# A two-layer hybrid decoder trunk: small matmuls of layer 1's head pairs regrouped between dense matmuls

## The reference

```python
p = h @ w_in
q = p[..., :768].reshape(B, S, 12, 64)
k = p[..., 768:1536].reshape(B, S, 12, 64)
v = p[..., 1536:2304].reshape(B, S, 6, 128)
q = rope(rmsnorm(q, q_norm), positions)
k = rope(rmsnorm(k, k_norm), positions)
...
# for each block of 128 queries, causal
s = einsum('bhqd,bhkd->bhqk', qblk, kh) * 64 ** -0.5
pr = softmax(s).reshape(B, 6, 2, 128, S)
a = pr[:, :, 0] - lam * pr[:, :, 1]
o = einsum('bhqk,bhke->bhqe', a, vh)
...
o = rmsnorm(o, subln) * (1.0 - lambda_init)
```

## Time and profile before

| what | us |
|---|---|
| median of 3 timed runs | 1314.48 (1314.1 to 1315.12) |
| the profiled execution | 1307.47 |
| its span | 1305.4 |
| TensorE busy | 1260.0, 97% |
| GpSimd busy | 722.3, 55% |
| VectorE busy | 609.6, 47% |
| ScalarE busy | 331.2, 25% |

### The profile page before, as it was taken

The page is one execution under the profiler, slowest core; times in us unless marked ns, Lnnn a source line. Parts: engine busy times, 40 slices in busy tenths (PEclk is TensorE's granted clock), DMA queues, the critical chain, the costliest instruction groups (busy, mean ns, idle before and its releaser), DMA issues.

```text
span 1305.4 us, 15225 instructions
## 1 busy us (share of the span) xinstructions
PE 1260.0 (97%) x5762; PEld 1008.4 (77%) x5762; DVE 609.6 (47%) x792; ACT 331.2 (25%) x659; POOL 722.3 (55%) x428
## 2 busy tenths in 40 slices
PE   8999999989999999999999999988999999999999
PEld 6787676658888888888887677766888888888887
DVE  6952522557434233313376888854743313331331
ACT  6422323462221001100122444455222101100110
POOL 6866522316666666666665434322666666666664
PEclk9999999989999999999999999988999999999999
DMA  6323211012323222322233232210222232233322
GB/s 247 97 97 99 95 33 49 33 33 97 105 96 97 97 96 96 97 97 96 77 102 112 65 98 65 82 33 25 97 88 96 96 97 96 96 96 97 97 76 100
DMA packets 34331, 115.85 MB, mean 89 GB/s; under 512 B 4333, under 2 KB 4846, under 8 KB 34158
## 3 DMA queue, kind: packets, MB, share of 16 engines
q1 hardware_dynamic: 32544, 111.16, 26.1%
q10 hardware_dynamic: 1742, 4.10, 1.1%
HBM read 110.00 MB, written 2.10 MB: 86 GB/s over the span
## 4 chain that ended last, share of the span: by engine, by line
PE 87%; DVE 7%; ACT 4%; issue 1%; POOL 1%; DMA 0%; ACTq 0%; SPq 0%; DVEq 0%; POOLq 0%
PE PS L1348 85%; DVE acc L912 2%; DVE nmB L1282 1%; POOL w_lo L467 1%; DVE nmB L1281 1%; DVE xT L1170 1%; DMA xT<-in_x_t_dram 0%; PE PS L1712 0%; DVE Al L1108 0%; ACT tmp L510 0%; DVE Hl L922 0%; ACTq L765 0%; ACT V L695 0%; DVE PS L1279 0%; POOL w_hi L464 0%
## 5 line engine op out<-in xcount | busy, mean ns | idle before, releaser
L464 POOL TENSOR_SCALAR w_hi<-w_raw 128x1024 fp32r<-128x1024 f32 (+1 forms) x205 | 215.5, 1051 | 551.3 <-PE PS L1348 550.7
L467 POOL TENSOR_TENSOR w_lo<-w_raw,w_hi 128x1024 fp32r<-128x1024 f32 (+1 forms) x205 | 499.1, 2435 | 17.1
L1348 PE MATMUL PS<-Hh,w_hi 128*128 128x512 f32 x1072 | 433.1, 404 | 10.8 <-POOL w_lo L449 6.2
L1348 PE MATMUL PS<-Hh,w_lo 128*128 128x512 f32 x1072 | 419.0, 391 | 0.0
L1348 PE MATMUL PS<-Hl,w_hi 128*128 128x512 f32 x1072 | 418.5, 390 | 0.0
L1348 PEld LDWEIGHTS PS<-Hh,w_hi 128*128 128x128 f32 x1072 | 201.8, 188 | 64.2 <-issue 18.3
L1348 PEld LDWEIGHTS PS<-Hh,w_lo 128*128 128x128 f32 x1072 | 201.7, 188 | 42.8
L1348 PEld LDWEIGHTS PS<-Hl,w_hi 128*128 128x128 f32 x1072 | 202.2, 189 | 38.0 <-issue 1.2
L1348 PE MATMUL PS<-Ah,w_hi 128*128 128x512 f32 (+1 forms) x544 | 207.0, 381 | 1.5 <-DVE Al L1213 0.9
L1348 PE MATMUL PS<-Al,w_hi 128*128 128x512 f32 (+1 forms) x544 | 205.5, 378 | 0.0
L1348 PE MATMUL PS<-Ah,w_lo 128*128 128x512 f32 (+1 forms) x544 | 205.4, 378 | 0.0
(11 more groups left out here) (251 smaller groups left out, 1006.3 us busy)
## 6 DMA issues: line engine op xcount, KB each, us to landing
w_raw<-in_wt_dram SPq DMA_DIRECT2D x189, 512.0 KB, 3.3
w_raw<-in_wt_dram SPq DMA_DIRECT2D x16, 384.0 KB, 3.1
QKR<-QKP ACTq DMA_DIRECT2D x24, 128.0 KB, 4.4
xT<-in_x_t_dram SPq DMA_DIRECT2D x8, 256.0 KB, 6.1
out_dram<-xT SPq DMA_DIRECT2D x8, 256.0 KB, 2.1
mT<-in_mem_t_dram SPq DMA_DIRECT2D x1, 1024.0 KB, 9.7
cn<-in_constants_dram ACTq DMA_DIRECT2D x1, 580.5 KB, 6.7
w_raw<-in_wt_dram SPq DMA_DIRECT2D x4, 128.0 KB, 6.2
```

The source lines that it names most:

```text
L464: nc.gpsimd.tensor_scalar(w_hi[:, sl, 0:nk], w_raw[:, raw, 0:nk], 0.0, 1.0, ALU.add, ALU.mult).then_inc(w_round, 1)
L467: nc.gpsimd.tensor_tensor(w_lo[:, sl, 0:nk], w_raw[:, raw, 0:nk], w_hi[:, sl, 0:nk].bitcast(F32), ALU.subtract).then_inc(w_split, 1)
L1348: return nc.tensor.matmul(out_, a, b, start=start, stop=stop)
```

## The change

Only the three functions that place the small pieces change; nothing is added or left out.

- `in_q`: the eight square sums stood in pairs behind steps 0, 1, 2 and 3, now all behind step 1, behind `b_t(c - 1, 3)`.
- `in_k`: the turns of the norm factors stood two by two behind steps 0 and 1, now all behind step 1; the turns of the output behind steps 2 and 3, now behind 3; the turns of v behind 5 and 6, now behind step 7, ahead of the scores of block 1.
- `in_v`: the scores of block 3 stood behind step 2, now behind step 4. It changes nothing for the last pair, which has no V tile.

```diff
                     if c >= 1 and k < 2:
                         b_t(c - 1, 2 + k)
-                    if k < NT:
-                        b_ss(c, 0, k)
-                        b_ss(c, 1, k)
+                    if k == 1:
+                        for a in range(2):
+                            for t in range(NT):
+                                b_ss(c, a, t)
                     if c >= 1 and k == 3:
                         b_pv(c - 1)
 
                 def in_k(k):
 
-                    if k < 2:
-                        b_kbc(c, 2 * k)
-                        b_kbc(c, 2 * k + 1)
-                    if c >= 1 and k in (2, 3):
-                        b_oturn(c - 1, 2 * (k - 2))
-                        b_oturn(c - 1, 2 * (k - 2) + 1)
+                    if k == 1:
+                        for t in range(NT):
+                            b_kbc(c, t)
+                    if c >= 1 and k == 3:
+                        for t in range(NT):
+                            b_oturn(c - 1, t)
                     if k == 4:
                         b_s(c, 0)
-                    if k in (5, 6):
-                        b_vt(c, 2 * (k - 5))
-                        b_vt(c, 2 * (k - 5) + 1)
                     if k == 7:
+                        for t in range(NT):
+                            b_vt(c, t)
                         b_s(c, 1)
 
                 def in_v(k):
 
-                    if k in (0, 2):
-                        b_s(c, 2 + k // 2)
+                    if k in (0, 4):
+                        b_s(c, 2 + k // 4)
                     if k in (5, 6):
                         b_t(c, k - 5)
```

## The result

| kernel | median, us | runs |
|---|---|---|
| before | 1314.29 | 4 (1311.8 to 1315.12) |
| after | 1331.4 | 4 (1330.73 to 1332.05) |

The medians lie 17.1 us apart. The ratio of the runs is 1.0137, which is 18.0 us, with a 95% interval of 1.0121 to 1.0152, or 15.9 to 20.0 us. The profiled execution of after took 1332.03 us, its span 1330.0. One run of the kernel before, made beside three of the later variants, fell into a slow state (1596.49 us at a mean clock of 0.743) and is left out of every ratio.

The account below looks back on a forecast made before the run. TensorE, busy for 97% of the span, was taken to bound the kernel. Waits +4.6 and clock +10.5 make +15.1 us: profiled 1307.47 becomes 1322.6, or 1329.5 with the timed runs' 7 us difference; range 1309 to 1337.

Parts of the forecast that it names:

- The likeliest case: Layer 1's head pairs get new stalls and the clock falls in nearly every pair: 1329.5 us, 1323 to 1337, chance 0.60.
- The wait that goes: V tile: TensorE's wait for ScalarE's exponentials ahead of block 3's scores goes in full, -1.31 us per pair.
- The gathering: Same small matmuls on TensorE in fewer groups: -0.1 us a pair, bounds -0.2 and +0.2.
- VectorE held twice: Block 3: GpSimd's w_hi holds line 1292 until about +11.08, then w_lo holds line 1293 until +13.3 to +13.6.
- The two new waits: TensorE waits ahead of block 2's transposes, 0.5 us, and ahead of block 3's transpose, 1.95 us, per pair.
- Sum without the clock: Gains and new waits per pair: +1.05 us, bounds +0.6 and +1.55; five pairs +5.2.
- Head and tail: The way to the first K tile's mark is 0.6 us shorter; nothing was put down for the tail behind the last.
- The clock: It falls once in nearly every pair, costing 2.1 us a pair, +10.5 in all; bounds +6 and +17.
- What leads to the fall: Idle times of 0.5 and 1.95 us, then 1.8 us of two-column matmuls; clock low from the square sums on.
- Rival 1: The stalls come in the pairs but the clock stays: +4.6 us, 1319 (1317 to 1322), chance 0.16.
- Rival 2: Line 1293 of block 3 is not held by w_lo: -0.9 us per pair, 1309.4 (1309 to 1314), chance 0.24.
- The point from which rival 2 decides: Whether line 1293 of block 3 takes the shared SBUF ports before w_lo does, at +11.1; a 0.04 us race.

Follow-up runs that it names:

- the PSUM variant: The kernel after, but line 1292 of block 3 writes to a free part of PSUM, from where the subtraction reads; 1307.74 us, ratio 0.9956.

## Why the prediction was right, and which term was too small

The likeliest case came true; 1331.4 us against 1329.5. Step by step:

- **The wait that goes: right.** The scores start at +6.08 (+6.1 predicted) without a wait.
- **The gathering: -0.1 a pair predicted, 0.0 measured.** The gathering alone shortens a pair by 0.47, and the wait for the scores by 0.46.
- **VectorE held twice: right, in each time.** w_hi at +9.78 (+9.8), its end at +10.99 (+11.0), line 1292 from +10.30 to +11.07 (+11.08), line 1293 from +11.10 (+11.12), 0.03 us behind w_lo's start, to +13.57 (+13.3 to +13.6). The step that no row showed, that line 1292 is held, is shown by after and by the PSUM variant.
- **The two new waits: right.** The transposes of block 2 follow the last dense matmul (794.94) by 0.78 instead of 0.23, so 0.5 late as predicted; the transpose of block 3 by 2.23 (796.42 to 798.65), so 2.0 late (1.95). The profile's idle times for them, 0.39 and 1.82, are less, since the records of the matmuls ahead end later than the pace of 0.23 says.
- **Sum without the clock: +1.05 a pair predicted, +1.2 measured** (-1.31 + 0.0 + 0.5 + 2.0), and 29.42 - 28.13 = +1.3 with the stall filled, which runs over by 0.1. Five pairs: 6.0 for 5.2.
- **Head and tail:** -0.5 measured for -0.6 in the head; the tail, for which nothing was put down, took 0.4 more.
- **The clock: the mis-sized term.** +10.5 us was predicted, from 2.1 a pair. Clock-free, a pair takes 28.13 + 1.2 = 29.33; the five take 1.64, 3.24, 3.08, 3.24 and 3.03 more, 14.2 us. That the clock falls in every pair was right, and that it costs half of TensorE's work in the stretch too: 3.2 us for 6.8 us at 0.53. But I had put weight on the shortest stretch of the rows, 3.4 us, and four of the five are twice as long. The bound of 3.4 a pair held. The trace of the kernel before could have said so: beside the two stretches of the earlier trace rows it has two of 6.8 us, in layer 0 from 264.9 and in layer 1 from 886.2. Most of the second:

```profile
886.30:892.90 6.60, 5.03 (x23) 4.63 (x24) 1.04 (x5) 6.35 (x19) 0.00 (x0) 0.50 0.00 0
```

- **What leads to the fall: right in part.** The fall was to come from the square sums on, with them as a part of its cause. It came among them in three pairs and ahead of them in two. And the new stretch doesn't have less in it than both rows of before: in the pair shown TensorE was busy for 1.53 us in the 3.40 ahead of the fall (794.90 to 798.30), against 1.18 and 2.07 in the earlier trace rows.

With the measured terms the sum is 6.0 + 14.2 - 0.5 + 0.4 = 20.1 us on the profile, 5 more than predicted, but the medians of the runs show 17.1. That the time came out within 2 us of the forecast is in part luck, since two deviations offset each other: the clock's term was 3.7 too low, and the 7 us between before's profile and its median were carried over whole. The profile of before had little low clock in layer 0; that of after lost 4.6 us more there and lies at its median. The record shows that the profile of before was a rare run: of the 13 runs of the same kernel made beside the first variants, 12 took 1311.8 to 1315.1 us at a mean clock of 0.981 to 0.986, and one 1307.37 us at 0.990, like the profiled one. Where the remaining 3 us lie stays open: only one execution of each kernel has a trace, and the loss differs from pair to pair, as the kernel with spread sums shows.

**The rivals.** Rival 1 (stall without clock) is the kernel with the filled stall: 1319.22 us, 1319 predicted. Rival 2 (line 1293 not held) is the one with PSUM: 1307.74, 1309.4 predicted, 27.32 us a pair for 28.13 - 0.9 = 27.23. So both were priced to within 2 us and neither happened. The point from which rival 2 decides was a race of 0.03 us in the pair shown; line 1293 lost it, and the wait behind it is 1.82 to 1.83 us in all five pairs.

## What to carry to other kernels

- A wait of the bounding engine can be what keeps two other engines apart. Before removing one, follow what the earlier end releases (here the split on GpSimd) and look at what it then meets.
- Where VectorE takes several times its usual time for a few elements, look at what GpSimd does in the same time. Passing one small operand through PSUM, or letting GpSimd wait for the last short operation, gave 24 and 22 us against after here; moving TensorE's work did not.
- Price a stall of TensorE with the clock that it may cost. Here 2.5 us of waits a pair cost 2.8 us of clock on top, and matmuls that nobody reads gave 12 us back.

## What the runs showed of the hardware beyond that

- The waits of a pair don't tell how long the clock stays low. Idle times of 0.34 to 0.39 and 1.82 us with the sixteen two-column records behind them led to 3.4 to 6.8 us at the lower level; 0.84 and 1.11 us, with such groups of four records between dense steps, to 10.2 us in four pairs and to none in the first, which has the same two (0.86 and 1.11 us). The single idle of 1.23 us a pair before, and single ones of 0.39 and 0.8 us in the variants, led to none.
- Between w_hi and w_lo there are 0.08 us. Line 1292, which was waiting by then, ended 0.08 behind w_hi, while line 1293, which needs that result, started 0.03 us behind w_lo and lost 2.1 us. To 0.01 us the recorded starts don't tell who goes first: with the gathering alone line 1293 starts at 787.88 and w_hi at 787.89, and line 1293 is held all the same (1.19 us).
- GpSimd waits in the same way: w_hi took 1.21 us instead of 1.04 where it met line 1293 of block 2 already running (in after, 794.80 and 794.62).
